# Last expert unit by column halves, with a final norm that starts on the left columns

## The reference

```python
def moe_ffn(h, w_router, b_router, w1, b1, w2, b2):
    ...                                   # top-4 of 32 experts per token, softmax weights
    def expert_block(args):
        tok, e = args
        xb = x_pad[tok]
        gu = xb @ w1[e] + b1[e]           # 1024 -> 2048
        gate = jnp.minimum(gu[:, :F], SWIGLU_LIMIT)
        up = jnp.clip(gu[:, F:], -SWIGLU_LIMIT, SWIGLU_LIMIT)
        act = (up + 1.0) * gate * jax.nn.sigmoid(SWIGLU_ALPHA * gate)
        return act @ w2[e] + b2[e]        # 1024 -> 1024
    ...                                   # outputs weighted and added to their tokens

x = x + moe_ffn(hf, ...)
y = x * lax.rsqrt(jnp.mean(x * x, axis=-1, keepdims=True) + 1e-5)   # final norm
out = y * norm_final_g
```

## Time and profile before

| | |
|---|---|
| median of three runs | 1231.49 us |
| profiled execution, its own time | 1230.75 us |
| its span, first to last instruction | 1228.7 us |
| PE busy | 1168.7 us (95%) |
| DMA, mean rate over the span | 376 GB/s |
| end of the last w2 row block on PE | 1219.62 us |
| end of the last scaling on DVE | 1226.26 us |

### The profile page before, as it was taken

The page is one execution under the profiler, slowest core; times in us unless marked ns, Lnnn a source line. Parts: engine busy times, 40 slices in busy tenths (PEclk is TensorE's granted clock), DMA queues, the critical chain, the costliest instruction groups (busy, mean ns, idle before and its releaser), DMA issues.

```text
span 1228.7 us, 17261 instructions
## 1 busy us (share of the span) xinstructions
PE 1168.7 (95%) x7138; PEld 584.6 (48%) x7138; DVE 427.1 (35%) x744; ACT 206.2 (17%) x303; POOL 58.6 (5%) x43
## 2 busy tenths in 40 slices
PE   9999999999999999999999999999999999899997
PEld 8888888888633333333333333333333333333332
DVE  5966765655722232222222222222222222222222
ACT  6444553534400000000000000000000000000001
POOL 0950000000300000000000000000000000000000
PEclk9999999999999999999999999999999999999999
DMA  9856437838999999999999999999999999999996
GB/s 312 267 207 224 152 137 269 310 140 350 409 428 427 429 428 428 428 429 428 429 428 428 429 428 428 428 428 429 429 428 428 429 428 429 428 429 429 428 425 281
DMA packets 57250, 462.31 MB, mean 376 GB/s; under 512 B 5761, under 2 KB 7490, under 8 KB 31906
## 3 DMA queue, kind: packets, MB, share of 16 engines
q1 hardware_dynamic: 53848, 458.97, 90.1%
q10 hardware_dynamic: 3370, 2.88, 0.8%
HBM read 459.71 MB, written 1.07 MB: 375 GB/s over the span
## 4 chain that ended last, share of the span: by engine, by line
PE 59%; DMA 37%; SPq 1%; ACT 1%; DVE 1%; issue 0%; DVEq 0%; ACTq 0%
DMA w_ring<-in_w 23%; PE ps L1241 15%; PE ps L1300 11%; DMA behind_watt<-in_w 7%; DMA behind_xb<-in_w 7%; PE ps L958 4%; PE ps L1390 3%; PE ps L966 3%; PE ps L964 3%; PE ps L965 3%; PE ps L1215 2%; PE ps L959 2%; SPq L578 1%; PE ps L978 1%; PE ps L1091 1%; PE ps L1093 1%
## 5 line engine op out<-in xcount | busy, mean ns | idle before, releaser
L1241 PE MATMUL ps<-w_ring,A_W 128*64 128x512 f32 x1232 | 278.1, 596 | 30.6 <-DMA w_ring<-in_w 29.1
L1830 DVE TENSOR_SCALAR A_W<-ps 128x512 f32<-128x512 f32 x32 | 22.1, 691 | 484.0 <-PE ps L1241 484.0
L1241 PEld LDWEIGHTS ps<-w_ring,A_W 128*64 128x64 f32 x1232 | 85.4, 137 | 205.8 <-issue 149.8
L1300 PE MATMUL ps<-w_ring,A_W 128*64 128x512 f32 x592 | 134.2, 595 | 0.0
L1472 DVE TENSOR_TENSOR w_parts<-w_ring,w_parts 128x1024 fp32r<-128x1024 f32 x76 | 110.0, 1466 | 57.2 <-ACT w_parts L690 56.3
L1241 PE MATMUL ps<-A_QK,A_W 128*64 128x512 f32 x416 | 94.2, 594 | 9.2 <-DMA A_QK<-in_w 8.7
L869 ACT ACTIVATE A_W<-ps 128x512 f32<-128x512 f32 x31 | 18.5, 597 | 438.3 <-PE ps L1281 438.3
L690 ACT ACTIVATE w_parts<-w_ring 128x1024 fp32r<-128x1024 f32 x75 | 78.9, 1058 | 64.7 <-PE ps L959 32.1
L865 ACT ACTIVATE A_W<-A_W 128x512 f32<-128x512 f32 x32 | 20.2, 630 | 394.8 <-DVE A_W L1830 394.8
L958 PE MATMUL ps<-hT_both,w_parts 128*128 128x512 f32 x224 | 79.3, 399 | 0.0
L1300 PEld LDWEIGHTS ps<-w_ring,A_W 128*64 128x64 f32 x592 | 40.4, 136 | 68.6 <-issue 66.9
(11 more groups left out here) (264 smaller groups left out, 1215.1 us busy)
## 6 DMA issues: line engine op xcount, KB each, us to landing
w_ring<-in_w SPq DMA_DIRECT2D x110, 2048.0 KB, 43.5
A_QK<-in_w SPq DMA_DIRECT2D x38, 2048.0 KB, 42.6
behind_watt<-in_w SPq DMA_DIRECT2D x19, 2048.0 KB, 43.5
w_ring<-in_w_in SPq DMA_DIRECT2D x36, 1024.0 KB, 7.4
behind_xb<-in_w SPq DMA_DIRECT2D x18, 2048.0 KB, 43.5
w_ring<-in_w SPq DMA_DIRECT2D x10, 1024.0 KB, 9.3
w_ring<-in_w_ret_branch SPq DMA_DIRECT2D x2, 2048.0 KB, 10.5
A_W<-in_w_out SPq DMA_DIRECT2D x1, 2560.0 KB, 13.2
```

Source lines behind the costliest of these rows:

```text
L1241: mm = pe.matmul(o, XT[:, k, :], tile[:, j, c * HALF:(c + 1) * HALF], start=(k == 0), stop=(k == KC - 1))
L1300: mm = pe.matmul(ps[CAP * c:CAP * c + CAP, 3, :], lhs, w2_tile(flat)[:, q % W2_ROWS, c * HALF:(c + 1) * HALF], start=False, stop=(q == FQ ...
L1830: dve.tensor_scalar(gl, bank(0), LIMIT, None, ALU.min).then_inc(s.g, 1)
```

## The change

The last unit is loaded and multiplied by column halves, and the final norm starts with the left columns.

- Loads: instead of four row blocks, SP loads all four row blocks of the left columns (1 MB, in 2 KB pieces), then the right columns of blocks 0 and 1 (512 KB), of block 2 (256 KB) and of block 3 (256 KB).
- PE: the four left products of the unit come first, alone; then expert 30's scatter to tile 0; then the right products of blocks 0, 1, 2; then expert 31's left scatter to tile 0; the right product of block 3; and the left scatter to tile 1 and the two right scatters.
- The two output halves of the last expert lie in two PSUM banks (`last_bank`), and DVE copies them apart.
- ACT squares four halves of 512 columns instead of two whole rows; DVE turns the left sum into a mean with the epsilon added, which is the bias of the root. DVE multiplies the left columns by the gain ahead of the root, and scales them by the reciprocal after it.

```diff
+        LAST_PIECES = [(slice(0, W2_ROWS), slice(0, HALF)), (slice(0, 2), slice(HALF, D)),
+                       (slice(2, 3), slice(HALF, D)), (slice(3, 4), slice(HALF, D))]
...
-            for j in range(W2_ROWS):
-                flat, _, _ = place(N_UNITS - 1)
-                sp.dma_start(w2_tile(flat)[:, j, :], w2_source(N_EXP - 1, 1)[:, j, :]).then_inc(s_quarter[j], 16)
+            last_unit, last_source = w2_tile(place(N_UNITS - 1)[0]), w2_source(N_EXP - 1, 1)
+            for n, (rows, cols) in enumerate(LAST_PIECES):
+                sp.dma_start(last_unit[:, rows, cols], last_source[:, rows, cols]).then_inc(s_quarter[n], 16)
...
             for t in range(TT):
-                act.wait_ge(*((s_scattered, N_EXP + 1) if t else (s_first, 1)))
-                act.activation(junk, bank(4 + 2 * t, 2), ACT.Square, accum_out=ssum[:, t:t + 1]).then_inc(s_sq, 1)
-                act.wait_ge(s_sq, 2 * TT + t + 1)
-                act.activation(ssum[:, t:t + 1], ssum[:, t:t + 1], ACT.Sqrt, bias=eps_col, scale=1.0 / D)\
+                act.wait_ge(s_first, t + 1)
+                act.activation(junk[:, t, 0, :], bank(4 + 2 * t), ACT.Square, accum_out=left_sum[:, t:t + 1]).then_inc(s_sq, 1)
+            for t in range(TT):
+                act.wait_ge(*((s_scattered, N_EXP + 1) if t else (s_first, 3)))
+                act.activation(junk[:, t, 1, :], bank(5 + 2 * t), ACT.Square, accum_out=ssum[:, t:t + 1]).then_inc(s_sq, 1)
+                act.wait_ge(s_means, 1)
+                act.wait_ge(s_sq, 3 * TT + t + 1)
+                act.activation(ssum[:, t:t + 1], ssum[:, t:t + 1], ACT.Sqrt, bias=left_mean[:, t:t + 1], scale=1.0 / D)\
                     .then_inc(s_root, 1)
...
-            def last_row(flat, q):
-                for c in range(2):
+            def last_bank(c):
+                return ps[CAP * c:CAP * c + CAP, 1 - c, :]
+
+            def last_row(flat, q, columns=range(2)):
+                for c in columns:
...
                 down_halves(2, i, 0, last_row)
                 flat, _, _ = place(w2_number(i, 1))
+                pe.wait_ge(s_quarter[0], 32)
                 for j in range(W2_ROWS):
-                    pe.wait_ge(s_quarter[j], 32)
-                    mm = last_row(flat, W2_ROWS + j)
+                    mm = last_row(flat, W2_ROWS + j, (0,))
+                mm.then_inc(s_left, 1)
+                scatter_tile(0, sc_w, y_sb)
+                for n in range(1, 4):
+                    if n == 3:
+                        pe.wait_ge(main.ye, N_EXP + 1)
+                        pe.wait_ge(main.swe, N_EXP + 1)
+                        scatter_columns(0, 0, last_sc, last_y).then_inc(s_first, 1)
+                    pe.wait_ge(s_quarter[n], 32)
+                    rows = LAST_PIECES[n][0]
+                    for j in range(rows.start, rows.stop):
+                        mm = last_row(flat, W2_ROWS + j, (1,))
                 mm.then_inc(s_used, 1)
...
             def scatter_last():
-                scatter_tile(0, sc_w, y_sb)
-                pe.wait_ge(main.ye, N_EXP + 1)
-                pe.wait_ge(main.swe, N_EXP + 1)
-                scatter_tile(0, last_sc, last_y).then_inc(s_first, 1)
-                scatter_tile(1, last_sc, last_y).then_inc(s_scattered, 1)
+                scatter_columns(1, 0, last_sc, last_y).then_inc(s_first, 1)
+                pe.wait_ge(main.ye, N_EXP + 2)
+                scatter_columns(0, 1, last_sc, last_y).then_inc(s_first, 1)
+                scatter_columns(1, 1, last_sc, last_y).then_inc(s_scattered, 1)
...
+            dve.wait_ge(s_left, 1)
+            dve.tensor_copy(last_y[0:CAP, :], ps[0:CAP, 1, :]).then_inc(main.ye, 1)
             dve.wait_ge(s_used, N_UNITS)
-            dve.tensor_copy(last_y, bank(1)).then_inc(main.ye, 1)
+            dve.tensor_copy(last_y[CAP:P, :], ps[CAP:P, 0, :]).then_inc(main.ye, 1)
...
-            for n, (t, h, cols) in enumerate(HALVES):
-                if h == 0:
-                    dve.wait_ge(s_root, TT + t + 2)
-                    link(dve.reciprocal(ssum[:, t:t + 1], ssum[:, t:t + 1]))
-                dve.scalar_tensor_tensor(xb[:, t, cols], bank(4 + 2 * t + h), ssum[:, t:t + 1], gain[:, cols],
+            left = slice(0, HALF)
+            dve.wait_ge(s_sq, 2 * TT + 1)
+            dve.tensor_tensor(xb[:, 0, left], bank(4), gain[:, left], ALU.mult)
+            dve.wait_ge(s_sq, 3 * TT)
+            dve.tensor_scalar(left_mean, left_sum, 1.0 / D, EPS, ALU.mult, ALU.add).then_inc(s_means, 1)
+            link(dve.tensor_tensor(xb[:, 1, left], bank(6), gain[:, left], ALU.mult))
+            for t in range(TT):
+                dve.wait_ge(s_root, TT + t + 2)
+                link(dve.reciprocal(ssum[:, t:t + 1], ssum[:, t:t + 1]))
+                dve.tensor_scalar(xb[:, t, left], xb[:, t, left], ssum[:, t:t + 1], None, ALU.mult).then_inc(s_fin, 1)
+                dve.scalar_tensor_tensor(xb[:, t, HALF:D], bank(5 + 2 * t), ssum[:, t:t + 1], gain[:, HALF:D],
                                          ALU.mult, ALU.mult).then_inc(s_fin, 1)
```

More of the change, by code:

```diff
@@ L198, in hybrid_block_kernel @@
         squares = A_W[:, 0:2048].rearrange("p (t d) -> p t d", t=TT)
-        junk = w2_flat[:, 0:D]
+        junk = w2_flat[:, 0:4 * HALF].rearrange("p (t c n) -> p t c n", t=TT, c=2)
         rest = A_W[:, 2048:4096].rearrange("p (t d) -> p t d", t=TT)
@@ L251, in hybrid_block_kernel @@
         ssum = small[:, 116:118]
+        left_sum, left_mean = small[:, 152:154], small[:, 154:156]
         rs_rest = small[:, 118:120]
@@ L377, in hybrid_block_kernel @@
         s_first = sem("first_tile_scattered")
+        s_left = sem("last_left_columns_done")
+        s_means = sem("left_mean_squares_ready")
         s_unit = [sem(f"ring_unit_loaded{j}") for j in range(RING)]
@@ L1345, in down_halves @@
                 mm.then_inc(s_used, 1)
-            def last_row(flat, q):
-                for c in range(2):
+            def last_bank(c):
+                return ps[CAP * c:CAP * c + CAP, 1 - c, :]
+            def last_row(flat, q, columns=range(2)):
+                for c in columns:
                     lhs = last_actT[:, (q % 4) * P + (q // 4) * CAP:(q % 4) * P + (q // 4) * CAP + CAP]
-                    mm = pe.matmul(ps[CAP * c:CAP * c + CAP, 1, :], lhs,
-                                   w2_tile(flat)[:, q % W2_ROWS, c * HALF:(c + 1) * HALF],
+                    mm = pe.matmul(last_bank(c), lhs, w2_tile(flat)[:, q % W2_ROWS, c * HALF:(c + 1) * HALF],
                                    start=False, stop=(q == FQ - 1))
@@ L1369, in down_last @@
                 for c in range(2):
-                    pe.matmul(ps[CAP * c:CAP * c + CAP, 1, :], sel2[0:BIAS_ROWS, :],
+                    pe.matmul(last_bank(c), sel2[0:BIAS_ROWS, :],
                               bias[:, 2 * F + c * HALF:2 * F + (c + 1) * HALF], start=True, stop=False)
@@ L1385, in project_down_extra, with scatter_columns @@
                         transpose_slots(extra, i)
+            def scatter_columns(t, c, weights, y):
+                rows = slice(CAP * c, CAP * c + CAP)
+                return pe.matmul(bank(4 + 2 * t + c), weights[rows, t * P:(t + 1) * P], y[rows, :], start=False,
+                                 stop=True, skip_group_check=True)
             def scatter_tile(t, weights, y):
[L1388 to L1392, removed]
+                scatter_columns(t, 0, weights, y)
+                return scatter_columns(t, 1, weights, y)
             def scatter(s, i):
```

## The result

The changed kernel takes 1235.47 us (median of 8 runs, 1235.23 to 1235.84), the kernel before 1231.3 us (8 runs). The ratio is 1.0034 with a 95% interval of 1.0024 to 1.0043: slower by 4.2 us, where I had said 4.4. Its profiled execution took 1235.23 us, 4.48 more than that of before; the sum had said 4.46.

The account below looks back on a forecast made before the run. Bounds: the transfers, unchanged in bytes, and the 10.2 us from last landing to the end. PE's +5.32 us less 0.86 from the tail made +4.46; on the timed scale 1231.49 + 4.4 = 1235.9 us, range 1234.3 to 1237.4.

Parts of the forecast that it names:

- A lone half costs two steps: PE, last unit: a left or right half multiplied alone takes 0.86 us, as long as a pair; lower bound 0.43 us.
- The switches: PE changing tile shape: 0.10 + 0.10 us into a scatter, 0.09 + 0.05 back; four ahead of the last row block, 0.68 us.
- full drains: PE's four tile-shape changes each costing a whole tail and fresh weight load: 0.5 us more; in a rival of 12%.
- PE's part: PE up to the end of the last row block: 1224.94 instead of 1219.62, +5.32 us.
- The start: PE's first left pass of the last unit at 1215.44, with 0.15 us more for loading 1 MB in 2 KB pieces.
- The tail: ACT and DVE after PE's last row block: the new norm gives back 0.86 us of the 5.32.
- The first (a lone half at half price): Rival, PE's last unit: a lone half costs half a pair; +0.14 us, about 1231.6, not slower; chance 6%.
- the late pieces: Rival, last unit's loads: left half lands 1 us later, PE starts 1 us later; 1236.4 to 1237.5 with full drains; chance 12%.
- My bound under gains: Whole kernel: even with half-price lone halves and free switches the end is near 1231.0; faster by over 0.2% gets 3%.

Follow-up runs that it names:

- partner kernel: The changed kernel, with a second, unread matmul of the same size beside each of the last unit's eight lone halves: 1235.8 us, 1.0037 times before.
- e_shift_moved: The kernel before, with 20 idle matmuls moved from the first group at the start into the second, keeping code positions: 1232.82 us, 1.0009 times before.

## Why the prediction was right

- *A lone half costs two steps.* 3.65 us for eight lone passes, as written down, and the added partners were free. The nearest rows, matmuls of other shapes without a partner, had the right price. Without them the page of before would have misled: PE's passes are as many in both kernels (7138) and its share is 95% in both. Only the busy time tells, afterwards: 1168.7 us before, 1174.1 in the changed kernel. The partner kernel has 16 passes more and the same 1174.1 us.
- *The switches.* The scatter began about 0.09 after the stream of the left halves had ended (1215.40 + 3.65 - 0.165) and took 1.13, and the way back began at 1220.03, about 0.09 after the scatter's stream. The range's allowance for full drains was not needed. The whole of PE's part came out at 5.25 us against 5.32.
- *The start.* The left half landed in time for 1215.40, 0.04 from the estimate. Whether the smaller pieces cost the 0.15 us taken for them can't be told: three executions with the same loads began the left half at 1215.40, 1215.61 and 1215.64.
- *A row misread, at no cost.* The prediction lists two waits of PE, at 1216.53 and 1218.54, that go. The first, 0.60 us, is of the weight loads only: PE's matmuls run through it (20 passes in 4.51 us). The sum uses neither.
- *The tail.* 0.91 us back instead of 0.86. DVE's gain products were done by 1227.48 and hidden.
- *The agreement to 0.02 us is luck.* The 4.46 are the shift of the last scaling, and that moved by 4.34 (5.25 - 0.91); about 0.15 more came between it and the end of the span (2.6 us, before 2.45), which the prediction had left as it was. The timed medians differ by 4.2, the profiled executions by 4.48; the interval of the ratio, 3.0 to 5.3 us, holds both.
- *The rivals.* The first (a lone half at half price) is refuted by eight lone passes in 3.65 us and by the partner kernel; the late pieces by the first pass at 1215.40, the drains by the gaps of 0.09. My bound under gains held: even with full pairs the idea gave no gain clear of the noise (0.5 us in the medians), though the rows of one stretch show 0.7.

## What to carry to other kernels

Before you take a product apart to have one part early, look at what its parts run beside: two halves that start within 0.01 us of each other are one price. When you separate them, the count of instructions stays and the busy share of the whole kernel hides it; here only PE's busy time rose, by 5.4 us. If you need an early part, cut it so that each piece still fills the array. And work moved ahead of a wait gains at most what lies behind the wait: here it gained 0.9 us of a tail of 6.6.

## What the runs showed of the hardware

The position of a loop in PE's code can cost 0.7%. With 8 instructions fewer ahead of it the loop of 5 experts (six turns) is loaded again in each turn, in 16 KB pieces (0.72 MB in 44 loads from 460 to 1180 us), and the kernel loses 8 us; with their place kept (e_shift_moved) it has no loads there. The Trainium skill, "Runtime: NRT & Kernel Launch", Instruction fetch mechanics, describes PE's instruction memory as 128 KiB, refilled in blocks of 16 KiB. The size of the loads agrees. The 45 loads more are nine for each of the five turns behind the first, and by the skill's two figures nine blocks are one more than the memory holds. That the loop lies in eight blocks from one start address and in nine from another would explain the step. For the kernel before, which loads nothing there, no run counts the blocks, so it stays a guess. The kernel before sits within 8 instructions of that step, so a count of the page's instruction queue belongs beside every time of it.
